# Two-block layer on one core: five early expert rows on other buffers, an unscaled first panel, and a redrawn order of work

## The reference, cut to what matters

```python
h = rmsnorm(x, norm1); proj = h @ w_in
qkv = causal_conv_silu(proj[q, k, v], conv_a)      # the first six weight panels
o_a = gated_delta_rule(...)                        # "delta0", "delta1": tile 0, tile 1
o_b = hgrn2_recurrence(...)                        # "hgrn0", "hgrn1"
x = x + (sig(g_a) * (o_a @ w_a) + sig(g_b) * (o_b @ w_b)) @ w_out
h2 = rmsnorm(x, norm2)
s = h2 @ w_pq against sub_keys; top 16 of 128 x 128 keys, for each of 8 heads
x = x + sum over the 128 chosen experts: gate * gelu(h2 . u[e]) * v[e]     # "rows"
x = rmsnorm(x, final_norm)
# second block: multiscale pooling, feed-forward, attention, feed-forward
```

## Time and profile before

| what | us |
|---|---|
| three runs, median (lowest to highest) | 1709.75 (1709.57 to 1715.63) |
| the profiled execution, its own time | 1710.97 |
| the profiled execution, span in the profile | 1709.1 |
| PE busy in the span | 1572.8 (92%) |
| DVE busy | 989.4 (58%) |
| ACT busy | 447.8 (26%) |
| POOL busy | 296.2 (17%) |
| first gather issued at; last one issued at | 407.2; 1103.9 |

### The profile page before, as it was taken

One profiled execution on the slowest core, in us unless ns is written; L12 is line 12 of the kernel. 1 busy time (PEld: TensorE's weight loads), 2 busy tenths in 40 slices (PEclk: granted clock), 3 DMA queues, 4 the chain that ended last, 5 costly groups with the idle time before them and its releaser, 6 DMA issues.

```text
span 1709.1 us, 21561 instructions
## 1 busy us (share of the span) xinstructions
PE 1572.8 (92%) x8696; PEld 1072.2 (63%) x8696; DVE 989.4 (58%) x1898; ACT 447.8 (26%) x1056; POOL 296.2 (17%) x271
## 2 busy tenths in 40 slices
PE   8999999999998889898689877789999999999998
PEld 7868888658554444375244322259995586599953
DVE  3354887317975664478957455445665415365654
ACT  1143342112554442233334222221000024210001
POOL 0000000001334444334446533300000000000000
PEclk9999999999999999999889999999999999999999
DMA  6364222378999999999999999983543523345432
GB/s 248 132 233 162 100 100 99 148 290 338 422 409 421 416 402 421 421 420 418 420 405 421 421 421 421 422 358 148 190 156 148 221 97 125 133 188 186 160 148 99
DMA packets 56798, 465.27 MB, mean 272 GB/s; under 512 B 6901, under 2 KB 8309, under 8 KB 10106
## 3 DMA queue, kind: packets, MB, share of 16 engines
q0 software_dynamic: 36864, 268.45, 38.0%
q1 hardware_dynamic: 19834, 195.43, 29.8%
HBM read 462.81 MB, written 1.05 MB: 271 GB/s over the span
## 4 chain that ended last, share of the span: by engine, by line
PE 59%; DMA 16%; DVE 8%; ACT 2%; issue 2%; POOL 0%; SPq 0%; DVEq 0%; ACTq 0%; POOLq 0%
DMA main<-in_expert_uv,main 15%; PE ps L2755 14%; PE ps L985 10%; PE ps L470 6%; PE ps L2909 6%; PE ps L1920 4%; PE ps L2675 3%; DVE main L913 2%; PE ps L2697 2%; PE ps L2984 2%; PE ps L2669 2%; PE ps L466 2%; PE ps L1251 1%; PE ps L229 1%; DMA panels<-in_wall 1%
## 5 line engine op out<-in xcount | busy, mean ns | idle before, releaser
L985 PE MATMUL ps<-main 128*128 128x512 f32 x820 | 381.2, 615 | 65.3 <-ACT main L960 65.1
L913 DVE SCALAR_TENSOR_TENSOR main<-main 128x1024 f32<-128x1024 f32 x220 | 264.3, 1223 | 147.4 <-DMA main<-in_expert_uv,main 147.0
L985 PEld LDWEIGHTS ps<-main 128*128 128x128 f32 x820 | 155.3, 196 | 274.9 <-issue 166.8
L895 POOL DMA_INDIRECT main<-in_expert_uv,main x220 | 248.5, 1130 | 384.4 <-PE ps L985 281.0
L2697 PE MATMUL ps<-xT,panels 128*128 128x256 f32 x576 | 125.8, 380 | 1.6 <-DMA panels<-in_wall 1.6
L2697 PEld LDWEIGHTS ps<-xT,panels 128*128 128x128 f32 x576 | 108.9, 190 | 17.2 <-DMA panels<-in_wall 1.9
L948 ACT ACTIVATE main<-main 128x2 f32<-128x2 f32 x128 | 25.9, 202 | 346.8 <-DVE main L913 300.8
L2755 PE MATMUL ps<-main 128*128 128x128 f32 x912 | 104.9, 275 | 0.0
L2755 PEld LDWEIGHTS ps<-main 128*128 128x128 f32 x912 | 103.4, 192 | 0.0
L470 PE MATMUL ps<-panels,main 128*128 128x512 f32 x192 | 83.6, 594 | 2.6 <-ACT main L499 2.6
L960 ACT ACTIVATE main<-mats,main 128x128 f32<-128x128 f32 x239 | 82.1, 387 | 0.4
(11 more groups left out here) (368 smaller groups left out, 2262.6 us busy)
## 6 DMA issues: line engine op xcount, KB each, us to landing
panels<-in_wall SPq DMA_DIRECT2D x69, 2048.0 KB, 7.9
panels<-in_wall SPq DMA_DIRECT2D x30, 1024.0 KB, 11.6
main<-in_rows SPq DMA_DIRECT2D x8, 512.0 KB, 9.6
main<-in_wall SPq DMA_DIRECT2D x4, 1024.0 KB, 12.5
main<-in_expert_uv,main POOLq DMA_INDIRECT x220, 15.4
main<-in_sub_keys SPq DMA_DIRECT2D x2, 1024.0 KB, 16.3
main<-in_wall SPq DMA_DIRECT2D x1, 2048.0 KB, 9.8
x<-in_x SPq DMA_DIRECT2D x2, 512.0 KB, 3.8
```

The source lines that it names most:

```text
L895: pool.indirect_dma_start(out=self.bufs[self.buf_of[r]], out_offset=None, in_=self.c.dram["expert_uv"], in_offset=bass.IndirectOffsetOnAxi ...
L913: dve.scalar_tensor_tensor(out=u, in0=u, scalar=1.0, in1=self.c.row(m, H2), op0=ALU.mult, op1=ALU.mult, accum_out=self.dots_at[:, m, q:q + ...
L985: mm = pe.matmul(self.c.ps[:, b, :], self.diags[self.of_pe(r) % DIAG_RING], v[:, half * HALF:(half + 1) * HALF], start=(q == 1), stop=(q = ...
```

## The change

1. `DELTA_FREE` goes from 0 to 5. The first five rows may no longer use the buffers 8 and 11 to 13; POOL waits for the end of the second delta rule before the sixth row and no longer before the first. The extra wait for `delta1.w` before the first row is gone.
2. The first weight panel is stored and loaded in two halves (256 columns each), the first behind x and the identity matrix, which is loaded between the two tiles of x. PE multiplies it by x that has the gain but not the token's scale (`first_products`), as soon as DVE has made that (L660 of the changed kernel); the two products that spread the scale stand between the halves; DVE multiplies the result by the scale as it copies it out, and makes the scaled `xT` for the other panels from the unscaled copy. Both sums of squares are now ACT's.
3. The pooling matrices are stored in three blocks of 128 x 128 and not as 128 x 256 rows; the block that is zero is no longer loaded. Tile 0's block is loaded where both loads stood, the two of tile 1 after the gathers, behind the first two panels of the feed-forward.
4. The list of `mixers_order` is redrawn: steps change places by a few positions, and the numbers in `rows(n)` change. `ADDED` has 19 rows in place of 17, among the first 20 rows 9 and 13 as well as 0.

```diff
-ADDED = [0, 41, 54, 58, 65, 67, 68, 73, 78, 85, 108, 128, 139, 158, 222, 242, 254]
+ADDED = [0, 9, 13, 21, 26, 28, 48, 53, 58, 67, 68, 69, 73, 81, 84, 101, 128, 177, 254]
...
-DELTA_FREE = 0
+DELTA_FREE = 5
...
-            if r == 0:
-                pool.wait_ge(*self.c.un.read_out("delta1.w"))
             if r == DELTA_FREE:
                 pool.wait_ge(*self.c.at("delta_done", 1))
...
-    for m in range(TILES):
-        sp.dma_start(c.x[:, m, :], c.dram["x"][m]).then_inc(c.x_loaded[m].sem, 16)
+    sp.dma_start(c.x[:, 0, :], c.dram["x"][0]).then_inc(c.x_loaded[0].sem, 16)
     sp.dma_start(c.mat("ident"), c.dram["mats"][:, MAT["ident"], :]).then_inc(c.ident_loaded.sem, 16)
+    sp.dma_start(c.x[:, 1, :], c.dram["x"][1]).then_inc(c.x_loaded[1].sem, 16)
     sp.dma_start(Project(c).gain, c.dram["norm1"]).then_inc(c.gain_loaded.sem, 16)
-    sp.dma_start(c.panels[:, 0, :], c.dram["wall"][0]).then_inc(c.panel_loaded[0].sem, 16)
+    first, second = slice(0, PANEL // 2), slice(PANEL // 2, PANEL)
+    sp.dma_start(c.panels[:, 0, first], c.dram["wall"][0][:, first]).then_inc(c.aside_loaded.sem, 16)
+    sp.dma_start(c.panels[:, 0, second], c.dram["wall"][0][:, second]).then_inc(c.panel_loaded[0].sem, 16)
...
+    pe.wait_ge(c.aside_loaded.sem, 16)
+    first_products(c, pe, 0)
     pe.wait_ge(*c.at("first_scale"))
...
+def first_products(c, pe, j):
+
+    t, w = Project(c), c.panels[:, 0, :].rearrange("p (j k n) -> p j k n", j=2, k=KC)
+    pe.wait_ge(c.bank_read[j].sem, c.bank_uses[j])
+    c.bank_uses[j] += 1
+    for n in range(2):
+        for k in range(KC):
+            if j == 0 and n == 0:
+                pe.wait_ge(*c.at("xT_made", 0, k + 1))
+            mm = pe.matmul(c.ps[:, j, n * T:(n + 1) * T], w[:, j, k, n * P:(n + 1) * P], t.unscaled[:, k, :],
+                           start=(k == 0), stop=(k == KC - 1))
+    mm.then_inc((c.half_done if j == 0 else c.panel_done).sem, 1)
...
-    for dst, src in ((t.mats[0], c.dram["pool_m"][:, 0]), (t.mats[1], c.dram["pool_m"][:, 1, :, P:T]),
+    for dst, src in ((t.mats[0], c.dram["pool_m"][:, 0]),
                      (t.pool_w, c.dram["pool_w"].rearrange("p g k n -> p (g k) n"))):
...
     c.restart(sp, "ff0")
+    sp.wait_ge(c.pool_loaded.sem, 16 * 2)
+    for n in (1, 2):
+        sp.dma_start(Second(c, 0).mats[n], c.dram["pool_m"][:, n]).then_inc(c.pool_loaded.sem, 16)
```

Two lines of the redrawn list, around the first choice of experts:

```diff
     part("tile0", "name0", "pq1", "scores2", "top1", "best1", "name1", "pq2", "pq3")
+    part("read1", 0)
+    part("tile0", "scores3")
     part("beside1", 0)
     rows(1)
```

More of the change, by code:

```diff
@@ L569, in project_tensor @@
     mm.then_inc(c.up("scale_spread"), 1)
-    for q in range(COUNT["conv"]):
-        products_of_both(c, pe, "conv", (q,), made="xT_made" if q == 0 else None)
+    c.panel_of(pe, "conv", 0)
+    first_products(c, pe, 1)
+    for q in range(1, COUNT["conv"]):
+        products_of_both(c, pe, "conv", (q,), made="xT_scaled" if q == 1 else None)
         if q == BT_BEHIND[0]:
@@ L596, in project_scalar @@
         act.sem_inc(c.pair_read[n].sem, 1)
-    act.wait_ge(*c.x_loaded[0].count(16))
-    act.activation(t.squared[:, 0, :], c.x[:, 0, :], ACT.Square,
-                   accum_out=t.squares[:, 0:1]).then_inc(c.up("first_square"), 1)
+    for m in range(TILES):
+        act.wait_ge(*c.x_loaded[m].count(16))
+        act.activation(t.squared[:, m, :], c.x[:, m, :], ACT.Square,
+                       accum_out=t.squares[:, m:m + 1]).then_inc(c.up("first_square"), 1)
     act.wait_ge(*c.at("scale_spread"))
@@ L604, in project_scalar @@
     for q in range(COUNT["conv"]):
-        for j in range(2):
+        for j in range(2) if q else ():
             bank = 2 * ((FIRST["conv"] + q) % 2) + j
@@ L648, in project_vector @@
             dve.sem_inc(c.bank_read[k // 2].sem, 1)
+    dve.wait_ge(*c.at("first_square", 0, 2))
+    dve.tensor_scalar(t.variance, t.squares, 1.0 / D, EPS, ALU.mult, ALU.add).then_inc(c.up("first_variance"), 1)
+    dve.wait_ge(*c.at("scales_kept"))
+    for k in range(KC):
+        dve.tensor_tensor(c.xT[:, k, :], t.unscaled[:, k, :], t.scales, ALU.mult).then_inc(c.up("xT_scaled"), 1)
+    for j in range(2):
+        wait_product(c, dve, "conv", 0, j)
+        dve.tensor_tensor(t.raw[:, 2 * j:2 * j + 2, 3:3 + T], c.ps[:, j, :].rearrange("p (k t) -> p k t", k=2),
+                          spread(t.scales, 2), ALU.mult).then_inc(c.bank_read[j].sem, 1)
+    dve.wait_ge(*c.at("zeros"))
     dve.wait_ge(*c.loaded.count(32))
@@ L2159, in mixers_order @@
     part("delta0", "P5")
[L2160 to L2161 removed]
+    beside(9)
+    part("sums0", "a1", "z1", "c1")
     part("delta0", "XY5")
+    part("hgrn0", "a2")
+    part("sums0", "w2", "x2")
     part("read0", 10)
[L2164 to L2165 removed]
     part("sums0", "y2")
+    part("hgrn0", "pick2", "both3")
+    part("sums0", "d1", "a2")
     part("delta0", "P6")
[L2168 removed]
+    part("hgrn0", "span4")
     part("beside0", 10)
+    part("sums0", "z2")
@@ L2195, in mixers_order @@
     part("sums0", "c3")
-    part("hgrn0", "both6")
+    part("delta1", "norm")
     part("sums0", "w4")
-    part("delta1", "norm", "turn")
-    part("sums0", "x4", "y4", "d3")
+    part("delta1", "turn")
+    part("sums0", "x4", "y4")
+    part("read0", 13)
+    part("sums0", "d3")
     part("beside0", 14)
-    part("read0", 13)
     part("delta1", "decay")
-    part("hgrn0", "a6")
     part("read0", 14)
-    part("hgrn0", "pick6")
+    part("hgrn0", "a6", "pick6")
     part("sums0", "a4")
+    part("hgrn0", "ends")
@@ L2221, in mixers_order @@
-    part("sums0", "d4")
     part("delta1", "P0")
     part("sums0", "a5")
-    part("delta1", "XY0")
-    part("sums0", "z5")
-    part("delta1", "v_t")
+    part("delta1", "XY0", "v_t")
     part("hgrn0", "gate")
@@ L2230, in mixers_order @@
     part("delta1", "XY1")
+    part("sums0", "z5")
+    part("read0", 18)
     part("sums0", "c5")
@@ L2339, in mixers_order @@
     part("hgrn1", "gate")
-    rows(69)
+    rows(70)
     part("tile1", "turn_a", "turn_b")
@@ L2343, in mixers_order @@
     part("tile1", "a")
-    rows(75)
-    rows(79)
+    rows(74)
+    rows(80)
     part("tile1", "b")
-    rows(85)
+    rows(81)
     part("tile1", "mix")
@@ L2352, in mixers_order @@
     part("tile1", "norm")
-    rows(100)
-    part("tile1", "pq0a", "scores0", "pq0b", "scores1")
-    rows(101)
-    part("tile1", "top0", "best0")
-    rows(105)
+    rows(97)
+    part("tile1", "pq0a", "scores0")
+    rows(98)
+    part("tile1", "pq0b", "scores1", "top0", "best0")
+    rows(104)
     part("tile1", "name0", "pq1")
```

247 lines of the change are left out of this document (115 added, 132 removed).

## The result

Six runs of the changed kernel have a median of 1717.02 us (1716.31 to 1722.81), six of the kernel before 1709.97 (1709.09 to 1715.63). The ratio is 1.0032, with a 95% interval of 1.0017 to 1.0047: 5.5 us slower, between 2.9 and 8.0. The profiled execution took 1716.31 us with a span of 1714.5, which is 5.4 us more than the span of before. Part of the nearness is luck, since the terms erred to both sides.

What follows compares the result with a forecast made beforehand. Transfers were taken to bound the gathers' stage (407 to 1135 us) and PE the stage before; +9.0 - 1.2 - 1.8 - 1.2 - 1.8 + 0 = +3.0 us on 1709.75 gave 1712.8 us, with an 8-in-10 range of 1703 to 1721.

Steps and rivals of the forecast that it cites:

- the hole: From 404 to 440 us, gathers waiting for PE's asides leave 3.8 MB unmoved: 9.0 us of DMA time lost.
- The bound: From 407 to 1135 us transfers bound the stage at 421 GB/s; DMA time with nothing queued is not given back.
- the rival of a refilled hole: Late gathers from 404 to 440 us are made up later at no cost: -6.0 us, 1703.8 us, chance 0.18.
- Row 24 and the gap at 490: Last expert names come near 503 us, queued rows just suffice, and the DMA gap at 490 us vanishes: -1.2 us.
- First panel: At the start, the half panel lets PE begin at 9.0 us and finish at 23.7, not 25.5: -1.8 us.
- Pooling matrices: In the gathers' stage, 0.52 MB less to load: -1.2 us, with 0 for the late load of tile 1's blocks.
- The gap at 890: Spreading products now in three places with rows between them close the DMA gap at 890 us: -1.8 us.
- Redraw: From 80 to 407 us only neighbouring steps change places: 0 us, bounds -6.5 and +3.
- the third rival: Refilled hole, and the new order takes PE's 6.5 us idle from 80 to 360 us: 1697.3 us, chance 0.08.
- The rival that asked for a second hole: Names of heads 6 and 7 come over 6 us later than 503, delaying row 24: 1721.5 us, chance 0.12.

Runs made afterwards that it cites:

- kernel 1: The changed kernel with the buffers of before (`DELTA_FREE` back to 0, the `delta1.w` wait restored): 1711.84 us, ratio 0.9988 to before.
- kernel 2: The kernel before with the changed buffers alone (`DELTA_FREE` = 5, no `delta1.w` wait): 1726.93 us, ratio 1.0077 to before.
- kernel 4: The kernel before with the redrawn order of work and the new `ADDED` list alone: 1712.54 us, ratio 0.9995 to before.
- kernel 3: The kernel before with the new first panel alone: ratio 1.0003 to before (0.9992 to 1.0014).
- kernel 7: The changed kernel with the buffers of before, plus 19 products of zeros on PE ahead of its first work: ratio 0.9980 to before.
- kernel 10: The kernel before with new first panel, 19 products of zeros, pooling blocks, and the new order only from row 133 on: 1708.31 us, ratio 0.9975.
- kernel 8: The kernel before with 24 products of zeros on PE alone, while it waits for its first data: ratio 0.9991 to before.
- kernel 5: The changed kernel with `DELTA_FREE` = 3, so the delta rule's buffers open from row 3: 1717.44 us, ratio 1.0029 to before.
- kernel 6: The changed kernel with the first aside's product ahead of the third and fourth key panels on PE: 1728.25 us, ratio 1.0095 to before.
- kernel 9: The kernel before with the three blocks of the pooling matrices alone: ratio 0.9994 to before (0.9986 to 1.0003).

## Why the prediction was right, and where it was not

The range of 18 us holds the measured time because the largest term, the hole, is right in mechanism and nearly in size. That it came within 2.5 us of the forecast is partly luck: the gains were put 3.9 us too high and the hole 1.5 us too high.

**The bound.** Right: from the feed-forward's panels to the end nothing moved by more than 1.2 us in any kernel (578.0 to 579.2), and what the DMA engines failed to move came out as time. Added up over the gathers' stage, the DMA time below 421 GB/s is about 7 us in before (I had said 8 to 9) and about 15 in the changed kernel, and the stage is 7.3 us longer.

**The hole, +9.0.** Right in mechanism, a sixth too large: 7.5 us by the ratios of the changed kernel and kernel 1. The second gather came at 425.23 and the fourth at 432.10, 1.9 and 2.8 us sooner than my 427.1 and 434.9: the first gather was already 1.9 us sooner, and to the fourth I had added 0.9 us for the scores although, as I said myself, the end of the second aside does not move by them. So 5.42 MB came in by 440 us, not 4.2. That both waits stand behind PE's asides, and that the waits for `delta_done` cost nothing, was as predicted. The dispute with the rival of a refilled hole is settled by kernels 1 and 2.

**Row 24 and the gap at 490, -1.2.** The names came just ahead of 504.50 us (I had said 503), but the margin did not quite hold and the gap did not vanish: 1.7 us are lost at 500 to 520, and kernels 1 and 4 have the same gap without the hole. Net 0 in place of -1.2.

**First panel, -1.8.** The mean of the executions says 1.8, the time of kernel 3 says +0.5 (-1.4 to +2.4), and in the two profiles compared it is 0.0. The step that failed is that a half panel takes 6.84 us: that row was taken after PE had risen to its faster level, and the new start puts the half panel where PE may still be at the slower one (8.90 us in the changed kernel). With PE at its faster level the forecast fits: the first panel ends at 23.66, 23.86 and 24.25 us in kernels 1, 7 and 10 with the new start, and at 25.87 and 25.16 in before and kernel 8 with the old one.

**Pooling matrices, -1.2.** Measured -1.0, not told from 0.

**The gap at 890, -1.8.** The gap closed, and the reason that I gave for it is not shown. The six kernels with the whole new order (changed, 1, 4, 5, 6 and 7) all move 421 GB/s from 780 to 920 us; the five with the old one (before, 2, 3, 8 and 9) move 416, 415, 419, 415 and 417, which is 0.7 to 2.0 us of DMA time. The same stretch of before, changed, 4, 8 and 9, in this order:

```profile
780.00:920.00 140.00, 111.82 (x256) 50.58 (x254) 107.47 (x266) 54.04 (x154) 64.24 (x56) 0.85 1.01 416
780.00:920.00 140.00, 114.63 (x295) 54.24 (x295) 109.08 (x289) 52.60 (x157) 68.39 (x57) 0.89 1.01 421
780.00:920.00 140.00, 114.68 (x274) 52.20 (x272) 107.12 (x270) 52.09 (x156) 68.39 (x60) 0.89 1.01 421
780.00:920.00 140.00, 106.36 (x253) 49.03 (x252) 108.10 (x259) 53.21 (x153) 64.12 (x57) 0.87 1.01 415
780.00:920.00 140.00, 112.04 (x304) 54.85 (x303) 110.47 (x272) 53.63 (x154) 66.12 (x55) 0.88 1.01 417
```

But I tied the gap to PE's spreading products at 868 us, from one execution. Kernels 8 and 9 keep the old order and have no gap behind these products (423 and 419 GB/s from 890 to 900); theirs stand ahead of them, at 830 to 850 us (375 and 379) and at 840 to 860 us (376 and 402). Kernel 10 has the products in three places, as the changed kernel does, but the old order up to row 133 and the old `ADDED`, and still moves only 417. PE's spreading products in the profile of before and in kernel 9 (shortest, median and longest of a record in ns):

```profile
L743 PE MATMUL ps<-to_spread,mats x24: 587/621/1052, 362.7 to 875.8; 5*128 5x512 f32 x24
```

```profile
L744 PE MATMUL ps<-to_spread,mats x24: 587/587/691, 366.2 to 879.5; 5*128 5x512 f32 x24
```

And the windows of before, where the granted clock is the third number from the end:

```profile
868.00:872.00 4.00, 4.00 (x9) 1.69 (x8) 0.12 (x1) 1.02 (x1) 2.77 (x3) 0.83 1.02 424
872.00:876.00 4.00, 4.00 (x6) 1.31 (x4) 0.00 (x0) 1.02 (x1) 0.00 (x0) 0.50 1.01 422
876.00:882.00 6.00, 0.85 (x1) 0.00 (x0) 1.62 (x4) 3.54 (x5) 0.00 (x0) 0.50 1.01 422
```

PE fell to 0.50 of its clock, its 1.2 GHz level, while still in the spreading products, so that these 12 records took 8.45 us; in kernel 8 the same 12 took 5.51 us, at 1.00 up to 872 us, and the fall came only near their end. That this made the rows and gathers behind late, and so put the gap of before at 890 us, fits the order of events and is not shown: in the changed kernel, too, 8 of these records took 4.46 us, as the clock fell (0.56 from 876 to 882 us), and no gap followed. So the -1.8 was right in size for this stretch. In the time of kernel 4 it does not stand out, because the stage loses DMA time elsewhere (the term of the redraw, below).

**Redraw, 0.** Measured -0.9 alone (-2.7 to +0.9), inside my bounds; this is the whole new order, with the gap at 890, for which I had -1.8. Kernel 4 gains 1.7 us from 780 to 920 us (421 GB/s against 416) and loses 1.9 from 600 to 660 (394 against 407). That last stretch is short of bytes in every kernel, by 1.4 us (kernel 1) to 5.0 (kernel 7), in either order. PE's 6.5 us of idle time from 80 to 360 us stayed (busy for 274.5 us in the changed kernel, 273.5 before), so the third rival falls. What I did not see is that the order works together with the buffers: without it they cost 13.2 us.

**The sum.** I had +9.0 and -6.0. Measured: +7.5 for the buffers in the new order, and -2.1 (-3.9 to 0.0) for all the rest together, which is kernel 1. That these two give 5.4, the measured 5.5, says nothing, since both ratios go through kernel 1. The test is the single measurements of the rest: +0.5, -0.9 and -1.0 add up to -1.4, near the -2.1 within their intervals. So my gains were 3.9 us too large (6.0 for 2.1) and the hole 1.5 us too large: 3.0 + 3.9 - 1.5 = 5.4. The step that failed is the booking of the small gains: of my -1.2 for the gap at 490 nothing came, of the -1.8 for the first panel nothing that the time shows, and of the -1.8 for the gap at 890, together with 0 for the redraw, -0.9. The rival that asked for a second hole is excluded for this kernel, and is what happens with the old order.

**Open.** Whether a later wait for row 3 alone would pay (kernel 5), and why the stages of kernels 1 and 7, the same instructions, differ by 3.7 us, was not settled. Where they differ can be read, kernel 1 first:

```profile
600.00:660.00 60.00, 55.43 (x155) 27.74 (x156) 36.39 (x53) 19.13 (x56) 26.50 (x19) 0.94 1.00 411
600.00:660.00 60.00, 52.47 (x144) 27.01 (x145) 36.08 (x52) 20.42 (x57) 27.33 (x19) 0.89 0.96 386
```

That is (411 - 386) x 60 / 421 = 3.6 of the 3.7 us. The granted clock differs there and in several other windows, but no run holds it fixed. Which part of the new order closes the gap between 780 and 920 us is open too.

## What to carry to other kernels

When transfers are the bound and one queue issues them in order, price a new wait by the bytes that can't be in flight behind it, and count also the queues that hang on the engine that is waited for: making the first wait short (kernel 6) made it worse, since SP's panels and the second wait moved with it. An order of work and a choice of buffers have to be measured together; here the first was worth 0.9 us alone and 6.6 with the second. And before a gap in one execution is booked as a gain, compare more than its own 10 us: in a second execution the same loss may stand 50 us earlier. Add up what is missing over the whole stretch, in several executions, before saying that a gap is closed or was never there.

## What the runs showed of the hardware that was not expected

PE begins an execution at its slower level (6 records of 128 columns per us, later 12), and in kernels with the same start the rise comes at different times, so that the first panel ends up to 3.6 us apart (23.7 to 27.3 with the new start, 25.9 to 28.8 in before and kernel 2). The clock column of the changed kernel's profile reads 1.00 from 9.5 to 20 us, through both rates; only the records' durations show the step. A fall later on does show in the column: in kernel 9 PE had been at its faster level at 9.99 us, waited 2.59 us, and the column reads 0.53 and 0.50 from 13 to 16 us, at 2 to 4 records per us. With some 20 products of zeros ahead of the first data the times are 1.4 and 1.5 us shorter by the ratios, each at the edge of what the runs can tell. In the gathers' stage PE also falls to 0.50, at a moment that differs between executions by a few us; where it fell early, 12 records took 8.45 us in place of 5.51.
